# The last token tile's modulated rows u: by Pool, a diagonal matmul and a plain store instead of VectorE, ScalarE and an adding store

## The chip, the cores and the metric

One Trainium2 chip, one core. A core has TensorE (PE, matmuls), VectorE (DVE), ScalarE (ACT), GpSimd (Pool) and SyncE (SP), each with its own instruction queue, and 16 DMA engines. They are ordered by semaphores alone: an instruction waits until a semaphore has reached a value, and instructions and DMAs raise semaphores when they are done. The metric is the time of one execution in microseconds, lower is better.

## What is computed

One layer of a hybrid backbone for 128 context tokens and 512 latent tokens: a modulated projection, three mixers (attention, a recurrence, a long convolution), an output projection with a norm, then a mixture of 16 experts of which each token takes two, and a last norm. The change lies between the first norm and the experts:

```python
xs = layer_norm(ALPHA * xs + g1 * mix, ln1_g[l], ln1_b[l])
u = layer_norm(xs) * (1.0 + sc2) + sh2
xs = layer_norm(ALPHA * xs + g2 * hier_moe(u, *moe_p), ln2_g[l], ln2_b[l])

def hier_moe(u, wg, bg, we, be, w_gate, w_up, w_down):
    g_logits = (jnp.einsum('bld,dg->blg', u, wg) + bg).astype(F32)
    g_idx = jnp.argmax(g_logits, axis=-1)
    ...
    e_logits = (jnp.einsum('bld,de->ble', u, we) + be).astype(F32)
    ...
    h = jax.nn.silu(jnp.einsum('bld,edf->blef', u, w_gate)) * jnp.einsum('bld,edf->blef', u, w_up)
    return jnp.einsum('blef,ble,efd->bld', h, combine, w_down)
```

Context tokens (c = 0) and latent tokens (c = 1) have their own sc2 and sh2.

## The kernel before

**Tiles.** The 640 tokens are TT = 5 tiles of P = 128 rows (tile 0 is context, tiles 1 to 4 latent), D = 1024 wide. The kernel is written engine by engine. The order on each engine is the order of the code, and there is no scheduler.

**Where u goes.** The experts read u row by row, gathered by token number. So each tile's u is written to a table in DRAM, u_scr (640 x 1024), and Pool then gathers the 128 rows of each expert from it with an indirect DMA (L895 in token_rows, into xg). TensorE turns the gathered rows (L1880), ScalarE and VectorE make a high and a low part of them, and the matmuls of the expert follow (L1898). SP's queue loads the experts' weights. Experts 0 and 1 are loaded early, and those of expert 2 wait until the first gather has landed (xg_in).

**How u is made.** X1 is the tile after the first norm, nmr its negative mean, rstd the reciprocal root of its variance, sc2b and sh2b the broadcast 1 + sc2 and sh2. Tiles 0 to 2: two passes on VectorE (L2473, L2474), and a plain store from Pool's queue (L867). Tiles 3 and 4 go another way: early in the stage (near 351 us) ScalarE's queue fills their rows of u_scr with sh2 (L1235). VectorE makes (X1 + nmr) * sc2 in one pass (scaled_rows, L2510) into u2_home[i], ScalarE multiplies by rstd (L1291, raises l1_std), and Pool's queue stores with an adding DMA (L889, raises scat).

```python
for i in range(TT - 2, TT):
    eng.wait_ge(l1_std, 2 * TT + i + 3 - TT)
    eng.dma_start(u_scr[i * P:(i + 1) * P, :], u2_home[i], accum_op=ALU.add).then_inc(scat, 16)
eng.wait_ge(scat, 16 * TT)
eng.wait_ge(slots_rdy, 1)
```

**The routing beside it.** The router's logits aren't made from u but from the rows turned before the second norm is applied: TensorE turns them (L1806), multiplies them with the router's weights (L1842, L1813), and turns the result (L1853, raises lg_mm to 3). VectorE corrects by mean and deviation (LOFF at L2520 and L2521, rr at L2522 for tile 4, by Pool at L880 to L884 for tiles 0 to 3), forms the logits LO (L2547, L2549), and goes on in some 40 small instructions, each waiting for the one before: group, ranks of the experts, the table of chosen experts (L2564, raises onehot). TensorE counts with it (L1859, L1861, raises rank_mm), VectorE makes one-hots of the ranks (L2584), TensorE turns them into token numbers (L1868), and L2599 writes the list tokens (raises slots_rdy to 1), by which Pool gathers. Where TensorE would idle, dense(n) puts n matmuls of 128x512 in between whose result nobody reads (L1833).

**ScalarE's order there:** the deviation of tile 4 (L1260, L1262), the copy of the logits (L1288), the two scalings (L1291), then eight gate_up_high, the high parts of the weights of experts 0 and 1 (L1256).

## Time and profile before

| | us |
|---|---|
| median of 3 runs | 634.61 |
| lowest and highest of them | 634.25, 636.15 |
| the profiled execution | 633.17 |
| its span in the trace | 631.3 |
| TensorE busy in the span | 600.8 (95%) |
| VectorE busy | 440.5 (70%) |
| ScalarE busy | 305.6 (48%) |
| Pool busy | 188.4 (30%) |

The span is the part of the execution that the trace covers. The 1.9 us around it are in every execution. Times in rows are microseconds from the span's start. "Idle before <- releaser" in a row says how long the engine stood still ahead of it and what ended that.

### The profile page before, as it was taken

To read this page: it belongs to the slowest core of one execution; us is meant where nothing else is said; L and a number is where in the kernel's file an instruction comes from. 1 tells how busy PE (TensorE), PEld (TensorE's weight loads), DVE (VectorE), ACT (ScalarE), POOL (GpSimd) and SP (SyncE) were. 2 spreads that over 40 slices of the span, in tenths; PEclk is the share of its full clock that TensorE was granted. 3 is DMA by queue.
4 is the path that set the end of the run, shared out by engine and by line. 5 is a ranking of instruction groups with operands and counts; after the bars stand their busy time and mean duration, and the time that the engine had idled before them with its cause. 6 is when DMAs were issued, how large, how long until landed. Compare 5 with 4: busy or idle time off the path is not lost.

```text
span 631.3 us, 9327 instructions
## 1 busy us (share of the span) xinstructions
PE 600.8 (95%) x3353; PEld 455.3 (72%) x3353; DVE 440.5 (70%) x757; ACT 305.6 (48%) x506; POOL 188.4 (30%) x152
## 2 busy tenths in 40 slices
PE   6899999999999988998999999989999999999994
PEld 2237999999999965557888888747767677676352
DVE  4967766834994654467553499988998877983187
ACT  2748122335344543005795342846565655752354
POOL 1002333345551307041496070421212221321121
PEclk9999999999999999999999999999999999999998
DMA  9985852222221269764980706769999999999788
GB/s 305 387 305 222 305 186 97 101 101 100 101 68 66 92 238 325 303 264 99 290 271 36 294 8 234 280 168 370 393 376 403 390 388 406 374 364 372 291 299 144
DMA packets 40040, 154.89 MB, mean 245 GB/s; under 512 B 7049, under 2 KB 17033, under 8 KB 27451
## 3 DMA queue, kind: packets, MB, share of 16 engines
q1 hardware_dynamic: 27912, 115.41, 50.6%
q10 hardware_dynamic: 5522, 23.48, 9.4%
q0 software_dynamic: 6560, 15.42, 8.3%
q8 instruction: 27, 0.44, 0.3%
q14 instruction: 19, 0.15, 0.1%
HBM read 141.59 MB, written 23.63 MB: 262 GB/s over the span
## 4 chain that ended last, share of the span: by engine, by line
PE 82%; DVE 7%; DMA 5%; ACT 4%; issue 2%; POOL 0%; DVEq 0%; ACTq 0%; POOLq 0%
PE bank L1898 13%; PE bank L1574 12%; PE bank L1575 12%; PE bank L1770 9%; PE bank L1952 8%; PE bank L1410 3%; PE bank L1747 2%; PE bank L1674 2%; PE bank L1880 2%; DMA arena<-in_w_mod 2%; PE bank L1477 2%; PE bank L1625 2%; PE bank L2011 2%; PE bank L1730 2%; DMA u_scr<-arena 1%
## 5 line engine op out<-in xcount | busy, mean ns | idle before, releaser
L772 POOL TENSOR_TENSOR w_low<-arena,w_high 128x1024 fp32r<-128x1024 f32 x22 | 53.6, 2437 | 145.9 <-ACT w_high L971 145.9
L2544 DVE TENSOR_TENSOR gate_up_low<-arena,gate_up_high 128x1024 fp32r<-128x1024 f32 x64 | 75.3, 1221 | 12.3 <-ACT gate_up_high L1256 10.2
L1256 ACT ACTIVATE gate_up_high<-arena 128x1024 fp32r<-128x1024 f32 x64 | 63.9, 1054 | 15.5 <-DMA arena<-in_moe_w_gu 15.5
L971 ACT ACTIVATE w_high<-arena 128x1024 fp32r<-128x1024 f32 x22 | 23.2, 1058 | 87.8 <-PE bank L1575 87.0
L1574 PE MATMUL bank<-u_high,w_high 128*128 128x320 f32 x176 | 56.3, 320 | 1.7 <-DVE u_low L2157 1.7
L1952 PE MATMUL bank<-arena 128*128 128x512 f32 x128 | 57.7, 593 | 0.0
L1575 PE MATMUL bank<-u_high,w_low 128*128 128x320 f32 x176 | 54.4, 309 | 0.0
L1574 PE MATMUL bank<-u_high,w_low 128*128 128x320 f32 x176 | 54.4, 309 | 0.0
L1574 PE MATMUL bank<-u_low,w_high 128*128 128x320 f32 x176 | 54.4, 309 | 0.0
L1575 PE MATMUL bank<-u_low,w_high 128*128 128x320 f32 x176 | 54.4, 309 | 0.0
L1575 PE MATMUL bank<-u_high,w_high 128*128 128x320 f32 x176 | 54.4, 309 | 0.0
L1898 PE MATMUL bank<-gate_up_high,xt_high 128*128 128x512 f32 x128 | 51.4, 402 | 0.5 <-DVE xt_low L2696 0.5
L1898 PE MATMUL bank<-gate_up_low,xt_high 128*128 128x512 f32 x128 | 50.0, 391 | 0.0
L1898 PE MATMUL bank<-gate_up_high,xt_low 128*128 128x512 f32 x128 | 50.0, 390 | 0.0
L902 POOL DMA_INDIRECT y_scr<-arena,store_rows x16 | 17.7, 1108 | 84.2 <-DVE arena L2710 79.7
L1952 PEld LDWEIGHTS bank<-arena 128*128 128x128 f32 x128 | 23.2, 190 | 23.1 <-issue 23.0
L895 POOL DMA_INDIRECT arena<-u_scr,tokens x18 | 19.6, 1087 | 59.1 <-PE bank L1880 49.6
L1574 PEld LDWEIGHTS bank<-u_high,w_high 128*128 128x128 f32 x176 | 33.1, 188 | 2.9 <-DVE u_low L2157 2.6
L1575 PEld LDWEIGHTS bank<-u_high,w_high 128*128 128x128 f32 x176 | 33.1, 188 | 0.2 <-issue 0.2
L1574 PEld LDWEIGHTS bank<-u_low,w_high 128*128 128x128 f32 x176 | 33.0, 188 | 0.0
L1574 PEld LDWEIGHTS bank<-u_high,w_low 128*128 128x128 f32 x176 | 33.0, 188 | 0.0
L1575 PEld LDWEIGHTS bank<-u_low,w_high 128*128 128x128 f32 x176 | 33.0, 188 | 0.0
(442 smaller groups left out, 1396.4 us busy)
## 6 DMA issues: line engine op xcount, KB each, us to landing
arena<-in_moe_w_gu SPq DMA_DIRECT2D x38, 1024.0 KB, 10.1
arena<-in_w_mod SPq DMA_DIRECT2D x24, 1024.0 KB, 6.6
arena<-in_moe_w_down ACTq DMA_DIRECT2D x13, 1024.0 KB
arena<-in_w_in SPq DMA_DIRECT2D x11, 1024.0 KB, 4.8
arena<-in_moe_w_down SPq DMA_DIRECT2D x6, 1024.0 KB
y_scr<-arena SPq DMA_DIRECT2D x11, 512.0 KB, 9.1
arena<-in_x SPq DMA_DIRECT2D x10, 512.0 KB, 9.6
arena<-y_scr SPq DMA_DIRECT2D x10, 512.0 KB, 6.0
```

The source lines that it names most:

```text
L772: G.tensor_tensor(WL[s_][:, :, w], ring[s_][:, :, w], WH[m % 2].bitcast(F), ALU.subtract).then_inc(wl_rdy, 1)
L895: eng.indirect_dma_start(xg[j], None, u_scr, bass.IndirectOffsetOnAxis(ap=which, axis=0), bounds_check=NTOK - 1, oob_is_err=False).then_in ...
L902: eng.indirect_dma_start(y_scr, bass.IndirectOffsetOnAxis(ap=stores[:, n:n + 1], axis=0), yy[n % 2], None, bounds_check=2 * NTOK, oob_is_e ...
L971: S.activation(WH[m % 2], ring[(m // 2) % 2][:, :, (m % 2) * P:(m % 2 + 1) * P], ACT.Copy).then_inc(wh_rdy, 1)
L1256: S.activation(WGH[j][c], raw_gu[s][:, c, :, :], ACT.Copy).then_inc(wgh_rdy, 1)
L1410: last = mm(bank[32 * g:32 * g + 32, :], cond32[k], w[:, 512 * g:512 * (g + 1)], start=(k == 0), stop=(k == KT - 1))
L1574: mm(B[1 + m % 2][:, 0:HALF], w, u[k][:, HALF:NTOK], start=first, stop=end)
L1575: last = mm(B[3 + m % 2][:, 0:HALF], w, u[k][:, 0:HALF], start=first, stop=end)
L1770: last = mm(B[2 * (i % 2) + b][:, :], x[j][:, k, :], w[p][c][:, k % 2, :], start=(k == 0 and q == 0), stop=(k == KT - 1 and q == 2))
L1898: last = mm(B[j][:, :], x[j][:, k, :], w[k // 2][:, k % 2, :], start=(k == 0 and q == 0), stop=(k == KT - 1 and q == 2))
L1952: last = mm(B[4 + b][:, :], hT[j][:, k, :], raw_dn[s][:, k, b * 512:(b + 1) * 512], start=(k == 0), stop=(k == 1))
L2544: tt_(WGL[s][c], raw_gu[s][:, c, :, :], WGH[j][c].bitcast(F), ALU.subtract).then_inc(wgl_rdy, 1)
```

## The change

For tile 4, the last one:

- VectorE's scaled_rows(4) goes. Pool makes (X1 + nmr) * sc2 in two halves of 512 columns, a tensor_scalar and a tensor_tensor for each (raising wcol_rdy to 4 and 5), between its work on the routing's corrections and its store of tile 3.
- ScalarE no longer scales the tile. It scales the 128x128 identity by rstd into root_diag.
- TensorE multiplies root_diag with each half and adds a row of ones times sh2 into the same bank, two matmuls for each half (raising lg_mm to 4 and 5). They stand where dense(4) stood. The next two groups of dense use banks 4 and 5 in place of 2 and 3.
- ScalarE copies each half from its bank to u2_home[4], one before its first gate_up_high and one before its second (raising l1_std to 2 TT + 4).
- SP stores the tile with a plain DMA (raising last_rows_st), ahead of the weights of expert 2. The filling of tile 4's rows of u_scr with sh2 goes, and so ld_late is waited for at 10.
- Pool stores tile 3 with an adding DMA as before, behind its four passes. The first gather waits for the four stores on scat, for last_rows_st, and for slots_rdy.
- Semaphore modc_in is dropped to make room, and cond_rdy counts to 2 in its place.

```diff
--- before.py
+++ after.py
@@ -308,6 +308,7 @@
         U2 = late.take(TT, D)
         YT = [late.take(KT, P) for _ in range(TT)]
         YTF = [y.rearrange("p a b -> p (a b)") for y in YT]
+        root_diag = U2[:, 0, 0:P]
         u2_home = [YTF[2], YTF[3], YTF[4], arena[:, MTH_AT[1]:MTH_AT[1] + D], U2[:, 4, :]]
         wr = Region(WO0 - 1216, 1216)
         WP = wr.take(2, KT, 20)
@@ -476,7 +477,7 @@
         out_st = sem("out_st")
         out_last = sem("out_last")
         scalar_st = sem("scalar_st")
-        modc_in = sem("modc_in")
+        last_rows_st = sem("last_rows_st")
         eo_win = sem("eo_win")
         ld_spec = sem("ld_spec")
         mask_in = sem("mask_in")
@@ -668,6 +669,8 @@
             eng.wait_ge(utl_rdy, KT + TT)
             for e in range(NE):
                 if e == 2:
+                    eng.wait_ge(l1_std, 2 * TT + 4)
+                    eng.dma_start(u_scr[4 * P:5 * P, :], u2_home[4]).then_inc(last_rows_st, 16)
                     eng.wait_ge(xg_in[0], 16)
                 gate_up_weights(e, e % 3, e * D)
                 if e == 0:
@@ -842,7 +845,7 @@
             out_low(3, 0)
             out_low(3, 1)
 
-            eng.wait_ge(ld_late, 16 * 11)
+            eng.wait_ge(ld_late, 16 * 10)
             eng.wait_ge(pv_mm, 40)
             by_row = [P, 2, KT, 20]
             wide = wrt.unsqueeze(1).to_broadcast(by_row)
@@ -883,11 +886,17 @@
             step(G.tensor_tensor(LOFF[:, most], LOFF[:, most], c4x[:, most], ALU.add))
             G.tensor_tensor(rr[:, most], r1s[:, most], rstd[:, most], ALU.mult).then_inc(wcol_rdy, 1)
             after(wcol_rdy)
-            eng.wait_ge(scat, 16 * (TT - 2))
-            for i in range(TT - 2, TT):
-                eng.wait_ge(l1_std, 2 * TT + i + 3 - TT)
-                eng.dma_start(u_scr[i * P:(i + 1) * P, :], u2_home[i], accum_op=ALU.add).then_inc(scat, 16)
-            eng.wait_ge(scat, 16 * TT)
+            eng.wait_ge(l1_var, 2 * TT)
+            eng.wait_ge(yt_mm, 2 * TT)
+            for b in range(2):
+                half = slice(512 * b, 512 * (b + 1))
+                step(G.tensor_scalar(u2_home[4][:, half], X1[:, 4, half], nmr[:, 4:5], None, ALU.add))
+                G.tensor_tensor(u2_home[4][:, half], u2_home[4][:, half], sc2b[:, 1, half], ALU.mult).then_inc(wcol_rdy, 1)
+                after(wcol_rdy)
+            eng.wait_ge(l1_std, 2 * TT + 2)
+            eng.dma_start(u_scr[3 * P:4 * P, :], u2_home[3], accum_op=ALU.add).then_inc(scat, 16)
+            eng.wait_ge(scat, 16 * (TT - 1))
+            eng.wait_ge(last_rows_st, 16)
             eng.wait_ge(slots_rdy, 1)
 
             def token_rows(j, which):
@@ -1231,8 +1240,7 @@
                 for c in range(2):
                     eng.dma_start(dst[:, c, :], mod_scr[c, m * D:(m + 1) * D].partition_broadcast(P)
                                   ).then_inc(ld_late, 16)
-            for i in range(TT - 2, TT):
-                eng.dma_start(u_scr[i * P:(i + 1) * P, :], mod_scr[1, D:2 * D].partition_broadcast(P)).then_inc(ld_late, 16)
+            eng.dma_start(u_scr[3 * P:4 * P, :], mod_scr[1, D:2 * D].partition_broadcast(P)).then_inc(ld_late, 16)
             for a, m in enumerate((2, 1)):
                 for c in range(2):
                     eng.dma_start(WCOL[:, 2 * a + c, :], mod_scr[c, m * D:(m + 1) * D].rearrange("(p k) -> p k", k=KT)
@@ -1286,10 +1294,14 @@
             deviation(TT - 1, 1)
             eng.wait_ge(lg_mm, 2)
             S.activation(LGT, B[1][:, 0:P], ACT.Copy).then_inc(yt_ev, 1)
-            for i in range(TT - 2, TT):
-                eng.wait_ge(u2_rdy, i + 1)
-                S.activation(u2_home[i], u2_home[i], ACT.Copy, scale=rstd[:, i:i + 1]).then_inc(l1_std, 1)
+            eng.wait_ge(u2_rdy, TT)
+            S.activation(root_diag, ident, ACT.Copy, scale=rstd[:, 4:5]).then_inc(l1_std, 1)
+            S.activation(u2_home[3], u2_home[3], ACT.Copy, scale=rstd[:, 3:4]).then_inc(l1_std, 1)
             for c in range(4):
+                if c < 2:
+                    half = slice(512 * c, 512 * (c + 1))
+                    eng.wait_ge(lg_mm, 4 + c)
+                    S.activation(u2_home[4][:, half], B[2 + c][:, :], ACT.Copy).then_inc(l1_std, 1)
                 gate_up_high(0, 0, 0, c)
 
 
@@ -1494,7 +1506,7 @@
             filter_layer(0)
             front_dense(4)
             filter_layer(1)
-            eng.wait_ge(modc_in, 1)
+            eng.wait_ge(cond_rdy, 2)
             front_dense(4)
             eng.wait_ge(filt_sin, 2)
             eng.wait_ge(ld_tables, 64)
@@ -1851,7 +1863,12 @@
             logits(4)
             eng.wait_ge(yt_ev, 2 * TT + 1)
             T.transpose(B[0][:, 0:P], LGT, ident).then_inc(lg_mm, 1)
-            dense(4)
+            eng.wait_ge(l1_std, 2 * TT + 1)
+            for b in range(2):
+                half = slice(512 * b, 512 * (b + 1))
+                eng.wait_ge(wcol_rdy, 4 + b)
+                mm(B[2 + b][:, :], root_diag, u2_home[4][:, half], start=True, stop=False)
+                mm(B[2 + b][:, :], ones[0:1, :], sh2b[0:1, 1, half], start=False, stop=True).then_inc(lg_mm, 1)
 
             eng.wait_ge(wcol_rdy, 2)
             eng.wait_ge(onehot, 1)
@@ -1861,7 +1878,7 @@
                 last = mm(counts[:, a + 1:, :], ones_w, MH[:, a, :].unsqueeze(1).to_broadcast([P, TT - a, NE]),
                           start=False, stop=(a == TT - 1))
             last.then_inc(rank_mm, 1)
-            dense(3)
+            dense(3, (4, 5))
             for q in range(2 * TT):
                 if q % TT == 0:
                     eng.wait_ge(onehot, 2 + q // TT)
@@ -1959,7 +1976,7 @@
             for i in range(TT):
                 last = mm(B[7][:, P + 2 * NE:P + 3 * NE], RO[:, TT + i, :], SECOND[:, i, :], start=(i == 0), stop=(i == TT - 1))
             last.then_inc(rank_mm, 1)
-            dense(5)
+            dense(5, (4, 5))
             rows_transposed(0, 0)
             dense(2, (4, 5))
             for n in range(NE):
@@ -2040,8 +2057,8 @@
             eng.wait_ge(ld_const, 16)
             eng.wait_ge(cond_rdy, 1)
             step(stt(sig, sig, 1.0, cond, ALU.add, ALU.mult))
-            ts_(cond, sig, 0.5, None, ALU.mult).then_inc(modc_in, 1)
-            after(modc_in)
+            ts_(cond, sig, 0.5, None, ALU.mult).then_inc(cond_rdy, 1)
+            eng.wait_ge(cond_rdy, 2)
 
             magic = 1.5 * 2.0 ** 23
             hi = 6.28125
@@ -2466,7 +2483,7 @@
 
                 c = 1 if i else 0
                 if i == 0:
-                    eng.wait_ge(ld_late, 16 * 11)
+                    eng.wait_ge(ld_late, 16 * 10)
                 if i < TT - 2:
                     eng.wait_ge(l1_std, 2 * i + 2)
                     step(V.reciprocal(rstd[:, i:i + 1], rstd[:, i:i + 1]))
@@ -2511,8 +2528,6 @@
 
             scaled_rows(3).then_inc(u2_rdy, 1)
             after(u2_rdy)
-            eng.wait_ge(yt_mm, 2 * TT)
-            step(scaled_rows(4))
             eng.wait_ge(l1_std, 2 * i + 2)
             V.reciprocal(rstd[:, i:i + 1], rstd[:, i:i + 1]).then_inc(u2_rdy, 1)
             after(u2_rdy)
```

Pool's queue between the routing's corrections (L882 to L884 before) and the first gather; arena is SBUF, u_scr the table in DRAM. Before:

```order
L882 TENSOR_TENSOR arena<-arena 128x80 [waits pool_step]
L883 TENSOR_TENSOR arena<-arena 128x80 [waits pool_step]
L884 TENSOR_TENSOR arena<-arena 128x4 [waits pool_step]
L889 DMA u_scr<-arena 128x1024 [waits l1_std,scat,wcol_rdy]
L889 DMA u_scr<-arena 128x1024 [waits l1_std]
L895 DMA arena<-u_scr,tokens 128x1024 [waits slots_rdy,scat]
```

Now:

```order
L885 TENSOR_TENSOR arena<-arena 128x80 [waits pool_step]
L886 TENSOR_TENSOR arena<-arena 128x80 [waits pool_step]
L887 TENSOR_TENSOR arena<-arena 128x4 [waits pool_step]
L893 TENSOR_SCALAR arena<-arena 128x512 [waits yt_mm,l1_var,wcol_rdy]
L894 TENSOR_TENSOR arena<-arena 128x512 [waits pool_step]
L893 TENSOR_SCALAR arena<-arena 128x512 [waits wcol_rdy]
L894 TENSOR_TENSOR arena<-arena 128x512 [waits pool_step]
L897 DMA u_scr<-arena 128x1024 [waits l1_std,wcol_rdy]
L904 DMA arena<-u_scr,tokens 128x1024 [waits slots_rdy,last_rows_st,scat]
```

Four passes stand ahead of the store of tile 3, and one of the two adding stores is gone.

VectorE in the same stretch, from the negative mean of tile 4 to the logits. Before:

```order
L2506 TENSOR_SCALAR arena<-arena 128x1 [waits vector_step]
L2510 SCALAR_TENSOR_TENSOR arena<-arena 128x1024 [waits l1_var]
L2510 SCALAR_TENSOR_TENSOR arena<-arena 128x1024 [waits yt_mm,u2_rdy]
L2517 RECIPROCAL arena<-arena 128x1 [waits l1_std,vector_step]
L2520 SCALAR_TENSOR_TENSOR arena<-arena 128x20 [waits wcol_rdy,u2_rdy]
L2521 SCALAR_TENSOR_TENSOR arena<-arena 128x20 [waits vector_step]
L2522 TENSOR_TENSOR arena<-arena 128x1 [waits vector_step]
L2547 TENSOR_TENSOR arena<-bank,arena 128x100 [waits lg_mm,ld_attn,vector_step]
L2549 TENSOR_TENSOR arena<-arena 128x100 [waits vector_step]
```

Now:

```order
L2523 TENSOR_SCALAR arena<-arena 128x1 [waits vector_step]
L2527 SCALAR_TENSOR_TENSOR arena<-arena 128x1024 [waits l1_var]
L2532 RECIPROCAL arena<-arena 128x1 [waits l1_std,u2_rdy]
L2535 SCALAR_TENSOR_TENSOR arena<-arena 128x20 [waits wcol_rdy,u2_rdy]
L2536 SCALAR_TENSOR_TENSOR arena<-arena 128x20 [waits vector_step]
L2537 TENSOR_TENSOR arena<-arena 128x1 [waits vector_step]
L2562 TENSOR_TENSOR arena<-bank,arena 128x100 [waits lg_mm,ld_attn,vector_step]
L2564 TENSOR_TENSOR arena<-arena 128x100 [waits vector_step]
```

One pass of 128x1024 is gone, and the rest stands as it did.

TensorE between the logits' last transpose and the counts. Before:

```order
L1813 MATMUL bank<-arena 128x20 x7
L1853 MATMUL bank<-arena 128x128 [waits yt_ev]
L1833 MATMUL bank<-arena 128x512 x4
L1859 MATMUL bank<-chosen,upper_whole 128x96 [waits onehot,wcol_rdy]
L1861 MATMUL bank<-chosen,ones_whole 128x80
```

Now:

```order
L1825 MATMUL bank<-arena 128x20 x7
L1865 MATMUL bank<-arena 128x128 [waits yt_ev]
L1870 MATMUL bank<-arena 128x512 [waits wcol_rdy,l1_std]
L1871 MATMUL bank<-arena 128x512
L1870 MATMUL bank<-arena 128x512 [waits wcol_rdy]
L1871 MATMUL bank<-arena 128x512
L1876 MATMUL bank<-chosen,upper_whole 128x96 [waits onehot,wcol_rdy]
```

Four matmuls that wait for Pool and ScalarE stand where four stood that waited for nothing.

## Rows read from the trace of the kernel before

**Rows 1.** The page: the span, and the chain that ended last by engine.

```profile
span 631.3 us, 9327 instructions
...
PE 82%; DVE 7%; DMA 5%; ACT 4%; issue 2%; POOL 0%; DVEq 0%; ACTq 0%; POOLq 0%
```

**Rows 2.** The chain in order of time, 396 to 425: start, duration, what.

```profile
406.83 0.78 POOL u_scr L889
407.61 8.44 DMA u_scr<-arena
...
416.08 0.04 POOLq L895
...
416.93 4.28 DMA arena<-u_scr,tokens
```

**Rows 3.** VectorE in order of time: start, duration, line, operation, operands, count, idle before.

```profile
403.16 2.61 DVE L2510 SCALAR_TENSOR_TENSOR arena<-arena 128x1024 f32<-128x1024 f32 x2
405.81 0.16 DVE L2517 RECIPROCAL arena<-arena 128x1 f32<-128x1 f32 x1
406.00 0.24 DVE L2520 SCALAR_TENSOR_TENSOR arena<-arena 128x20 f32<-128x20 f32 x1
...
406.56 0.16 DVE L2522 TENSOR_TENSOR arena<-arena 128x1 f32<-128x1 f32 x1
406.75 0.26 DVE L2547 TENSOR_TENSOR arena<-bank,arena 128x100 f32<-128x100 f32 x1
407.05 0.27 DVE L2549 TENSOR_TENSOR arena<-arena 128x100 f32<-128x100 f32 x1
...
415.44 0.23 DVE L2599 TENSOR_SCALAR tokens<-arena 128x16 int32<-128x16 f32 x1
```

**Rows 4.** Pool and VectorE side by side, 399 to 402, in order of time.

```profile
399.79 1.45 DVE L2501 SCALAR_TENSOR_TENSOR arena<-arena 128x1024 f32<-128x1024 f32 x1
...
399.81 0.35 POOL L881 TENSOR_TENSOR arena<-arena 128x80 f32<-128x80 f32 x1
400.24 1.18 POOL L882 TENSOR_TENSOR arena<-arena 128x80 f32<-128x80 f32 x1
```

**Rows 5.** ScalarE in order of time, 404 to 415.

```profile
404.63 0.29 ACT L1262 ACTIVATE arena<-arena 128x1 f32<-128x1 f32 x1
...
405.13 2.18 ACT L1291 ACTIVATE arena<-arena 128x1024 f32<-128x1024 f32 x2
407.21 7.67 ACT L1256 ACTIVATE gate_up_high<-arena 128x1024 fp32r<-128x1024 f32 x8
```

**Rows 6.** TensorE in order of time; an f32 matmul is two records.

```profile
406.25 0.31 PE L1853 MATMUL bank<-arena 128*128 128x128 f32 x1
406.39 3.60 PE L1833 MATMUL bank<-arena 128*128 128x512 f32 x8
410.75 0.20 PE L1859 MATMUL bank<-chosen,upper_whole 128*128 128x96 bf16 x1 [0.76 <-DVE chosen L2564]
```

**Rows 7.** Pool's groups by form: count, busy us, mean ns, idle before.

```profile
L803 POOL TENSOR_TENSOR arena<-arena 128x1024 f32<-128x1024 f32 x8 | 18.8, 2355 | 21.6 <-DMA arena<-in_rpb 21.5
...
L814 POOL TENSOR_TENSOR arena<-arena 128x256 f32<-128x256 f32 x10 | 7.3, 728 | 43.0 <-DVE arena L2351 43.0
...
L784 POOL TENSOR_SCALAR arena<-arena 128x1280 f32<-128x1280 f32 x1 | 1.3, 1267 | 0.1
```

**Rows 8.** Pool and VectorE at 111 us, in order of time.

```profile
111.66 2.42 POOL L772 TENSOR_TENSOR w_low<-arena,w_high 128x1024 fp32r<-128x1024 f32 x1 [5.17 <-ACT w_high L971]
...
111.78 2.31 DVE L2296 TENSOR_TENSOR arena<-arena 128x4 f32<-128x4 f32 x1
```

**Rows 9.** Landing of L867's plain and L889's adding stores; busy us by stretch, clock, DMA share.

```profile
DMA to landing us min/median/max: 2.9/3.4/7.1
...
DMA to landing us min/median/max: 6.3/7.4/8.4
...
405.00:410.00 5.00, 4.99 (x22) 2.72 (x21) 4.42 (x18) 5.00 (x6) 1.83 (x2) 1.00 1.02 351
410.00:415.00 5.00, 3.57 (x22) 1.63 (x22) 4.54 (x14) 4.98 (x7) 0.00 (x0) 1.00 0.97 178
```

## Prediction

> **What bounds the kernel now.** I read the page first, then the chain of waits through the routing stage, then each engine's rows of that stage in order of time. The page shows a kernel that TensorE bounds over most of its span: PE holds 82% of the chain that ended last [rows 1]. The change touches none of that bulk. It lies in the 20 us in which TensorE has nothing large to do, because the first expert's tokens aren't known yet. There the chain [rows 2] goes from ScalarE's scaled rows to Pool's adding store (issued at 407.61), to its landing 8.44 us later, and to the gather of the first expert's rows, which starts at 416.93 and lands 4.28 us later. Everything behind the gather waits for it: TensorE's transposes, the expert matmuls, and the next weights on SP's queue, which wait for the gather too. So a shift of the first gather passes on in full, and the forecast is the question of when that gather starts.
>
> Two things must be there before it: u in DRAM (semaphore scat) and the token list (slots_rdy). The chain names only the later one. VectorE's rows [rows 3] show the other: L2599 writes the list from 415.44 for 0.23 us, so it is there at **415.67**. The store's landing at 407.61 + 8.44 = 416.05 is only **0.38 us** behind it. That is the most that any faster store can give while VectorE's chain stays where it is.
>
> **What leaves VectorE.** One pass of 128x1024 (the second of the two at L2510, 2 x 1.30 us in one row [rows 3]) goes. The reciprocal L2517 stood at 405.81 behind it. It now waits for ScalarE's root, which starts at 404.63 and takes 0.29 us [rows 5], so it runs at about 404.97 to 405.13. That is 0.8 us earlier. The gain isn't kept: L2547 reads the transposed logits, and TensorE makes them at 406.25 to 406.56, behind a queue of its own that the change doesn't touch [rows 6]. VectorE came there at 406.75 in before. So without any new wait the list could come 0.2 us sooner at most.
>
> **What comes to Pool, and what it does to VectorE.** Pool gets four passes of 128x512: twice a tensor_scalar, then a tensor_tensor. The price of a tensor_tensor: 2355 ns at 1024 elements and 728 at 256 [rows 7], a slope of 2.12 ns, so 512 cost 1.27 us. For the tensor_scalar the nearest row is 1267 ns at 1280 elements with two constants [rows 7], about 0.53 us at 512. Here the scalar is a column of SBUF, which no row of Pool shows, so its upper end is the tensor_tensor's 1.27 us and its lower end 0.53. I take the lower, since the row is the same instruction with as many operands streamed. Sum: 2 x (0.53 + 1.27) = 3.6 us, up to 5.1.
>
> These passes aren't free for VectorE, though it waits on none of them by semaphore. At 111.66 Pool starts a tensor_tensor of 2.42 us, and VectorE's addition of 4 elements, started at 111.78, takes 2.31 us: it ends when Pool's does [rows 8]. Its like takes 0.16 (L2522 has one element [rows 3]). It works the other way as well: Pool's L882 starts at 400.24, takes 1.18 us in place of L881's 0.35, and ends 0.15 us after VectorE's 128x1024 pass (399.79 + 1.45 = 401.24) [rows 4]. An instruction of VectorE with two tensors in SBUF and one of Pool take turns, each holding off the other for its whole length. The routing chain consists of such small instructions.
>
> The page "SBUF — State Buffer" of the Trainium skill, section "SBUF: two separate sides", calls it an exclusive lock that whoever starts first keeps for the whole instruction, and exempts a VectorE instruction with only one tensor in SBUF. The 2.31 us above agree with the lock. By the exemption L2547, which reads one tensor from PSUM, would pass beside Pool, which moves the result between my two ends below and not beyond them.
>
> So the new order of time from 403 on, by these durations. Pool is ready at about 403.2, when the negative mean is there, as is VectorE's first L2510 (403.16 [rows 3]), which holds it until 404.45. Tensor_scalar until 405.0, tensor_tensor to 406.3, tensor_scalar to 406.9, tensor_tensor 407.0 to 408.3. VectorE's L2520 is ready at 405.2 and is held to 406.3. L2521 and L2522 get in between Pool's passes one at a time, and whichever is next at 407.0 is held to 408.3. If that is L2549 (started 407.05 in before, ended 407.32), it ends at about 408.4: **1.1 us** late. If it is still L2522, then L2522, L2547 and L2549 follow one another after 408.3 (0.1 + 0.3 + 0.3 us) and L2549 ends at about 408.95: **1.6 us** late. I take **1.3**. From there on nothing of Pool runs beside the chain, and its rest takes what it took: list at 415.67 + 1.3 = 417.0.
>
> **TensorE.** dense(4), 3.60 us of filling from 406.39 [rows 6], goes. In its place stand four matmuls of 128x512 in f32, as dense's were, so 3.6 us again, in two pairs of 1.8: from 406.6 (its first half is ready at 406.3) to 408.4, and from 408.4 to 410.2. The counts behind them waited for the one-hot until 410.75, which now comes 1.3 us later. So the matmuls are hidden with 1.8 us of room, and TensorE idles about 1.8 us there in place of 0.76. Without that cover they would be on the path with their whole length.
>
> **The store of the last tile.** ScalarE: diagonal 405.2 to 405.5, tile 3 scaled to 406.6 (1.05 us, as in before [rows 5]). It copies half 0 at 408.4 to 409.0, then one gate_up_high (1.0), then half 1 at 410.3 to 410.9. The other seven gate_up_high end at 417.6 in place of 414.88 [rows 5]. Their first reader on VectorE comes after the gather's issue, the first tile's pieces are done by 414, and the exponential behind them is needed only experts later: nothing. SP has nothing ahead of the plain store (its next weights wait for the gather), so it goes out at 410.9. The weights in front of it have drained by then (351 GB/s in 405 to 410, 178 in 410 to 415 [rows 9]). The plain stores of the other tiles land in 2.9 to 7.1 us, median 3.4 [rows 9], so **413.8 to 418.0**, and I take 414.5, since one adding store runs beside it.
>
> **The adding store of tile 3** stood ready at 406.28 and was issued at 406.83. Now it stands behind Pool's four passes: 408.3. The two adding stores landed in 6.3 and 8.4 us [rows 9], sharing the engines with each other and the weights. That gives 414.6 with the shorter and 416.7 with the longer. I take the shorter, as there is now one and the weights are out. Both stores are in before the list at 417.0: the list is what ends last.
>
> **Sum.** Gather released at 417.0 in place of 416.05: **+0.9 us** (+0.7 to +1.2 over the two ends of VectorE's delay). The other edits are at nothing: one preset of 512 KB fewer on ScalarE's queue near 352, under the output matmuls, the renamed wait at the start (same producer, same place), and the dense groups moved to other banks. The profiled execution took 633.17 us with a span of 631.3, so the same execution would take 634.1. The median of the runs shown lies 1.44 us above it, at 634.61, which gives **635.5 us**.
>
> **Rivals.** (a) *No turns taken:* VectorE's small instructions slip through Pool's passes. Then the list comes at 415.5 and both stores are in before it: -0.5 us, 634.1. For: Pool's L881, started 0.02 us behind VectorE's long pass, took only 0.35 us [rows 4]. Against: the 2.31 us for 4 elements [rows 8], the plainest row of the argument. (b) *Pool's passes run long*, slower than before. With the column operand at 1.27 us each, Pool ends 1.5 us later, at 409.8, and VectorE's delay grows to 2.6 to 3.1, the gather's to 2.2 to 2.7: 637.1. It passes 0.3% when Pool's sum exceeds about 4.6 us. Half 1's matmuls then end at 411.6, still before the one-hot. (c) *A store ends last:* the plain store at 7.1 us lands at 418.0, +1.95 us, 636.6. It decides once it takes over 6.1 us. For: it crosses an adding store; against: two of the three plain stores took 3.4 or less. (d) *The route is swapped but the gather isn't moved:* the store's 0.4 us and VectorE's delay cancel, 634.6; it needs a delay of only 0.4 us.
>
> The page "GPSIMD Engine Reference" of the Trainium skill, section "Elementwise — side-by-side cycle accounting", gives some 2.6 cycles of 1.2 GHz an element with two inputs and 1.03 for the simplest bodies. Worked out from it as an estimate, the four passes take 2 x (1.11 + 0.44) = 3.1 us without overhead, and the delay of VectorE would be about 0.5 us less, with a result near 635.0.
>
> **Chances.** Forecast (its +0.7 to +1.2, with 0.2 us to either side for the order in which the two engines take turns) 0.56, (a) 0.12, (b) 0.11, (c) 0.09, (d) 0.12. A measurement of this kernel tells about 0.3% from no change, 1.9 us. The forecast, (a) and (d) lie within it. (b) mostly and (c) in half its cases lie beyond, 0.15 with some of the forecast's tail. 0.04 is left for a gain beyond what any step here allows. The range takes in (a) and (b) with the 0.4 us by which the fastest of the runs shown lies below its median: 633.7 to 637.6.
>
> **What would show it.** Right: L2520's successor on VectorE (a pass of 20 elements, 0.24 us now) lasting over 1 us and ending with a tensor_tensor of Pool, Pool's passes summing to 3.6 us behind a held first one, onehot about 1.3 us later, and the wait before the gather naming VectorE's tokens and not a store. Wrong: routing instructions at their old 0.2 us beside Pool's passes, a tensor_scalar far over 0.53 us, or a store's landing as the gather's releaser. The granted clock falling in the 1.8 us of idle TensorE (it is 1.00 in the rows of this stretch [rows 9]) would add time that no term here holds.

## The result and the profile after

The change made the kernel slower. Over 8 executions each, the changed kernel took 639.69 us (median, 638.14 to 641.01) and the kernel before 634.46 (633.58 to 637.58), a ratio of 1.0065 with a 95% interval of 1.0042 to 1.0088. The forecast was 635.5 us with a range up to 637.6, "no change that can be told" as the likeliest: it was wrong. The profiled execution took 639.83 us with a span of 637.8, against 633.17 and 631.3.

The chain of waits through the routing stage of the changed kernel (start, duration, what):

```profile
403.74 2.59 POOL arena L893
406.33 0.07 issue
406.40 1.28 POOL arena L894
407.68 0.14 issue
407.81 2.01 PE bank L1870 x2
409.83 2.00 PE bank L1871 x2
411.83 2.00 PE bank L1870 x2
413.83 2.00 PE bank L1871 x2
415.83 0.19 PE bank L1876
...
423.51 4.31 DMA arena<-u_scr,tokens
```

The first gather starts at 423.51 and not at 416.93 [rows 2], 6.6 us later, and the span grew by 6.5. So in these two profiled executions the loss is all ahead of that gather. Neither a store nor VectorE holds it: the chain goes through Pool's first half and then through the four new matmuls, 2.0 us each where dense's took 0.9 [rows 6].

TensorE in order of time shows why. Its last transpose of the logits stands at 406.67, which is 0.42 us later than in before. That part came in ahead of this stage (in the profiled execution of the changed kernel TensorE's clock was also below full between 20 and 40, at 0.95 and 0.88, and in that of before it was not), and I leave it out of the account below.

```profile
406.67 0.30 PE L1865 MATMUL bank<-arena 128*128 128x128 f32 x1
407.81 2.01 PE L1870 MATMUL bank<-arena 128*128 128x512 f32 x2 [0.84 <-POOL arena L894]
409.76 2.07 PE L1871 MATMUL bank<-arena 1*128 1x512 f32 x2
411.76 2.08 PE L1870 MATMUL bank<-arena 128*128 128x512 f32 x2
413.76 2.07 PE L1871 MATMUL bank<-arena 1*128 1x512 f32 x2
415.77 0.26 PE L1876 MATMUL bank<-chosen,upper_whole 128*128 128x96 bf16 x1
415.83 0.40 PE L1878 MATMUL bank<-chosen,ones_whole 128*128 128x80 bf16 x5
416.08 5.47 PE L1845 MATMUL bank<-arena 128*128 128x512 f32 x6
```

The counts (L1876) had their one-hot from 412.13 on (L2579 below) and started at 415.77, behind the matmuls. The filling behind them (L1845, six records) took 5.47 us against 2.8 at full clock. The busy time by stretch names the cause. Its columns are the stretch, its length, busy us of PE, PEld, DVE, ACT and POOL with their instructions, the granted clock, the DMA share and GB/s:

```profile
400.00:405.00 5.00, 4.86 (x90) 4.28 (x88) 4.70 (x7) 4.97 (x11) 4.38 (x6) 1.00 1.00 416
405.00:410.00 5.00, 4.16 (x20) 2.50 (x21) 3.39 (x14) 2.02 (x5) 4.73 (x4) 0.78 0.87 364
410.00:415.00 5.00, 5.00 (x6) 1.25 (x6) 3.30 (x11) 1.54 (x2) 1.62 (x2) 0.50 0.53 75
415.00:420.00 5.00, 5.00 (x12) 2.14 (x12) 2.67 (x6) 4.13 (x5) 0.00 (x0) 0.50 0.41 135
420.00:425.00 5.00, 4.14 (x22) 1.69 (x21) 2.19 (x7) 4.80 (x7) 1.19 (x2) 0.85 0.00 0
```

**TensorE's clock fell from 2.4 to 1.2 GHz** between 405 and 410 and stood at half through 410 to 420, in a stretch in which before had 1.00 throughout ([rows 9] up to 415, and its trace up to 425). It isn't one bad execution: the mean granted clock of the eight, each over its whole span, was 0.982 to 0.988.

Pool and VectorE in the same stretch:

```profile
403.74 2.58 POOL L893 TENSOR_SCALAR arena<-arena 128x512 f32<-128x512 f32 x1 [0.31 <-DVE arena L2523]
406.40 1.27 POOL L894 TENSOR_TENSOR arena<-arena 128x512 f32<-128x512 f32 x1
407.77 1.56 POOL L893 TENSOR_SCALAR arena<-arena 128x512 f32<-128x512 f32 x1
409.42 1.26 POOL L894 TENSOR_TENSOR arena<-arena 128x512 f32<-128x512 f32 x1
```

```profile
405.65 0.24 DVE L2535 SCALAR_TENSOR_TENSOR arena<-arena 128x20 f32<-128x20 f32 x1
...
407.40 0.38 DVE L2564 TENSOR_TENSOR arena<-arena 128x100 f32<-128x100 f32 x1
...
408.03 0.46 DVE L2550 TENSOR_TENSOR arena<-arena 128x20 f32<-128x20 f32 x1
...
409.75 1.03 DVE L2574 TENSOR_TENSOR arena<-arena 128x80 f32<-128x80 f32 x1
...
411.89 0.24 DVE L2579 TENSOR_TENSOR chosen<-arena 128x80 bf16<-128x80 f32 x1
```

Three instructions of the routing chain are longer than their like (0.27, 0.18 and 0.24 us), by 0.11, 0.28 and 0.79 us. The first and the last end 0.1 us behind Pool's two tensor_tensors (407.67 and 410.68). L2535 took its usual 0.24 us, although Pool's first tensor_scalar ran until 406.32. Pool's two tensor_scalars took 2.58 us (held until VectorE's long pass ended at 404.87) and 1.56, not 0.53.

The stores, once they were issued, were quick. Pool's adding store of tile 3 (issued at 410.99) and SP's plain store of tile 4 (issued at 416.49):

```profile
DMA to landing us min/median/max: 5.4/5.4/5.4
...
DMA to landing us min/median/max: 2.6/2.6/2.6
```

The plain store landed at 419.1, and the list was there only at 422.55.

**Account of the 6.6 us**, with the 0.4 of shift taken out (6.2): the counts came 4.6 us late (415.77 against 410.75), of which VectorE's one-hot explains 1.1 (412.13 against 410.60) and the slow, late matmuls 3.5. From the counts to the list another 1.9 us, the filling matmuls at half clock. Less the 0.4 us by which the store had been later than the list in before.

### The profile page after: what moved, and what is told of

Same layout as the page of the kernel before. It is cut to its first block, busy times and chain, and to the rows that moved or that the text cites. A ratio compares the mean times of both kernels' runs of the same rounds, so it can differ in the third digit from the quotient of the medians.

```text
span 637.8 us, 9332 instructions
## 1 busy us (share of the span) xinstructions
PE 608.4 (95%) x3353; PEld 457.4 (72%) x3353; DVE 440.7 (69%) x756; ACT 306.5 (48%) x508; POOL 192.9 (30%) x155
## 4 chain that ended last, share of the span: by engine, by line
PE 82%; DVE 8%; DMA 3%; ACT 3%; issue 2%; POOL 1%; DVEq 0%; POOLq 0%; ACTq 0%
PE bank L1915 13%; PE bank L1586 12%; PE bank L1587 12%; PE bank L1782 9%; PE bank L1969 8%; PE bank L1422 3%; PE bank L1759 2%; PE bank L1686 2%; PE bank L1897 2%; PE bank L1489 2%; DMA arena<-in_w_mod 2%; PE bank L1637 2%; PE bank L2028 2%; PE bank L1742 2%; PE bank L1503 1%
```

## The experiments

The first theory: the idle 0.84 us ahead of the first new matmul, behind small matmuls, let the clock fall. The rival: something in the new work does. "One-row" in the table means that a matmul sums over one row of both operands (`1*128`, `1x512` in its row), "full" that it sums over 128, and "gap" an idle stretch ahead of the new or held matmuls. "Clock" is the range of the mean granted clock over the executions of a kernel. The kernel before has 0.987 to 0.997 in these series, and a ratio is to the kernel before on the same chip. The clock is a mean over the whole span, so it also holds what happened elsewhere: in the profiled executions of a4_const, b2_one_row and d1_pool_rows it was below full between 20 and 40 too, in code that b2 and d1 share with the kernel before. Only a trace tells where it fell, and there is one for each kernel (two for the changed one).

| kernel | TensorE in the stretch | median us | ratio, 95% | clock |
|---|---|---|---|---|
| changed | gap, one-row | 639.69 | 1.0065 (1.0042 to 1.0088) | 0.982 to 0.988 |
| a6_again (the same) | gap, one-row | 639.87 | 1.0078 (1.0054 to 1.0101) | 0.982 to 0.988 |
| a1_fill | filled, one-row | 635.83 | 1.0020 (0.9998 to 1.0042) | 0.987 to 0.996 |
| a2_full | gap, full | 636.32 | 1.0007 (0.9985 to 1.0028) | 0.991 to 0.997 |
| a5_two_ops | short gap, full | 635.59 | 1.0002 (0.9976 to 1.0028) | 0.988 to 0.996 |
| c1_vector_rows | no gap, one-row | 635.55 | 1.0005 (0.9976 to 1.0034) | 0.982 to 0.994 |
| c2_vector_rows_full | no gap, full | 635.06 | 1.0005 (0.9986 to 1.0023) | 0.989 to 0.997 |
| b1_gap | gap, dense | 634.91 | 1.0013 (0.9990 to 1.0036) | 0.986 to 0.996 |
| b2_one_row | no gap, one-row | 636.92 | 1.0029 (1.0008 to 1.0050) | 0.982 to 0.991 |
| b3_gap_one_row | gap, one-row | 638.21 | 1.0056 (1.0029 to 1.0084) | 0.980 to 0.991 |
| d1_pool_rows | no gap, dense | 637.98 | 1.0050 (1.0027 to 1.0074) | 0.989 to 0.997 |
| a4_const | filled, full | 637.11 (one execution) | | 0.990 |

**a1_fill: a filling matmul where TensorE stood idle.**

```diff
+            dense(1, (4, 5))
             eng.wait_ge(l1_std, 2 * TT + 1)
             for b in range(2):
```

> The changed kernel with one filling matmul (0.9 us, two records) ahead of the wait for Pool's first half, where TensorE stood idle 0.84 us. Theory 1 (the idle stretch behind the small matmuls of the logits let the clock fall to 1.2 GHz): the clock stays at 1.00 through 405 to 425, the four new matmuls take 3.6 us, not 8.0, the counts wait for the one-hot again, and the gather starts about 1.1 to 1.5 us later than in the kernel before: 635.6 to 636.1. Theory 2 (the clock falls with the new matmuls or with Pool's passes whatever stands ahead of them): it falls again, and the time stays near 639.5. Theory 3 (the lateness of Pool's second half alone costs it): the clock stays, yet the time is over 638.

635.83 us, a mean clock of 0.992 or more in nine of ten executions, the gather at 417.36. An idle stretch of 0.78 us ahead of the second half stayed, and both one-row matmuls. Theory 1 passed, and it looked settled. What ends last there is the plain store (issued at 412.40, landed at 416.45), 0.4 us behind the list. So in this trace Pool's lateness alone, at full clock, costs about a microsecond (the gather is 0.4 us later than in before, and the transpose of the logits 0.8 us earlier).

**b1_gap: the same idle stretch in the kernel before.**

```diff
+            eng.wait_ge(l1_std, 2 * TT + 2)
             dense(4)
```

> The kernel before with its dense(4) held until ScalarE has scaled both tiles, at about 407.3, so that TensorE stands idle some 0.75 us behind the logits' transpose as in the changed kernel, and nothing else is altered. Theory 1: the clock falls to 1.2 GHz at about 407, dense(4) takes near 8 us, the counts come 4 to 5 us late: 638 to 640. Theory 2 (the new matmuls or Pool's passes are needed for it): the clock stays at 1.00, dense(4) ends at 411.0 instead of 409.99, and the counts come 0.2 us late: 634.4 to 635.0.

TensorE stood idle for 0.80 us and dense(4) then took 3.70 us at full clock. 634.91 us, ratio 1.0013 with 1 inside the interval. **Theory 1 fell**: the gap by itself does nothing that can be told.

**c1_vector_rows: Pool's passes out, VectorE makes the rows again, TensorE's new work stays.**

```diff
-                step(G.tensor_scalar(u2_home[4][:, half], X1[:, 4, half], nmr[:, 4:5], None, ALU.add))
-                G.tensor_tensor(u2_home[4][:, half], u2_home[4][:, half], sc2b[:, 1, half], ALU.mult).then_inc(wcol_rdy, 1)
...
+            eng.wait_ge(yt_mm, 2 * TT)
+            step(scaled_rows(4))
...
+            eng.wait_ge(u2_rdy, TT)
-                eng.wait_ge(wcol_rdy, 4 + b)
```

> The changed kernel with Pool's four passes taken out and tile 4's scaled rows made by VectorE again in one pass, as in the kernel before. The diagonal, the row of ones and the plain store stay. Theory 1: the first half is there at about 406.3, before TensorE is done with the logits, so there is no idle stretch and no fall of the clock. VectorE's chain is as in the kernel before, the plain store lands at about 415, and the gather waits for the list: 0.3 to 0.5 us faster than before, 634.0 to 634.3. Theory 2 with the new matmuls as the cause (a fall with TensorE's new work): near 638. A plain store that takes over 5 us to land would end last and give 635 or more.

TensorE has no idle stretch here, and yet, in its order of time:

```profile
406.33 0.31 PE L1858 MATMUL bank<-arena 128*128 128x128 f32 x1
406.56 1.13 PE L1863 MATMUL bank<-arena 128*128 128x512 f32 x2
407.61 1.12 PE L1864 MATMUL bank<-arena 1*128 1x512 f32 x2
408.66 1.86 PE L1863 MATMUL bank<-arena 128*128 128x512 f32 x2
410.45 2.07 PE L1864 MATMUL bank<-arena 1*128 1x512 f32 x2
```

The first pair runs at full clock and the second at half: the clock fell in the middle of busy work. The executions spread from 633.54 to 640.72, with mean clocks from 0.982 to 0.994. My expectation of no fall was wrong, and the spread pointed at the new matmuls, of which every second has a single row of weights. The median of 635.55 is that of before: one-row matmuls without an idle stretch ahead of them cost nothing here that can be told, and only the spread and the trace speak.

**d1_pool_rows: Pool's part alone, in the kernel before.** Pool's four passes ahead of the adding stores, VectorE's pass out, ScalarE scaling behind Pool.

```diff
+                step(G.tensor_scalar(u2_home[4][:, half], X1[:, 4, half], nmr[:, 4:5], None, ALU.add))
+                G.tensor_tensor(u2_home[4][:, half], u2_home[4][:, half], sc2b[:, 1, half], ALU.mult).then_inc(wcol_rdy, 1)
...
+                if i == TT - 1:
+                    eng.wait_ge(wcol_rdy, 5)
...
-            step(scaled_rows(4))
```

> The kernel before with tile 4's scaled rows made by Pool's four passes, ahead of its two adding stores. ScalarE's scaling, the adding store and dense(4) stay. This is Pool's part alone. The clock stays at 1.00, since dense(4) waits for nothing (theory 1), or falls if Pool's passes were its cause (theory 2, 637 or more). Pool ends at about 410.3 by the 1.56 and 1.27 us of the changed kernel's passes, ScalarE at 411.4, the adding store of tile 4 goes out at 412 and lands 5 to 6.5 us later at 417 to 418.5, past the list (about 416.9, VectorE held for 1.2 us in all): the gather starts 1 to 2.5 us late, 635.6 to 637.0.

The clock stayed at 1.00 through 400 to 415, so Pool's passes do not pull it down there. It fell behind that, to 0.75 in 415 to 420 and 0.90 in 420 to 425, with no one-row matmul in the stretch; the gather was waiting for a store until 420.40, and TensorE then waited for the rows, so it cost nothing there. The one-hot was there at 411.74 against 410.60, so VectorE's chain came 1.1 us late, though it had one long pass less. The time, 637.98, is beyond my 637.0. In the profiled execution (637.89) that is the adding store of tile 4, which took 8.57 us to land and not 5 to 6.5:

```profile
411.83 8.57 DMA u_scr<-arena
```

Adding stores kept to the 8.4 us of [rows 9], and being one store behind the other seems to have mattered more than the emptier engines (DMA share 0.63 and 0.69, against 1.02 and 0.97).

**c2_vector_rows_full and a2_full: all 128 rows in place of one.**

```diff
-                mm(B[2 + b][:, :], ones[0:1, :], sh2b[0:1, 1, half], start=False, stop=True).then_inc(lg_mm, 1)
+                mm(B[2 + b][:, :], ident, sh2b[:, 1, half], start=False, stop=True).then_inc(lg_mm, 1)
```

> The kernel of c1_vector_rows with the row-of-ones matmul (one row of weights, sh2 from one row) replaced by the identity times the broadcast sh2, a matmul over all 128 rows with the same result. In c1 the clock fell at about 409 though TensorE never stood idle. Theory A (a matmul of one row counts for little activity, and the fall needs weak work, not idleness): the clock stays at 1.00 in 405 to 425, the four matmuls take 3.6 us, the gather waits for the list or the plain store, whichever is later, at about 415.5 on the time axis of the kernel before: 0.3 to 0.6 us less than before, and no execution near 638. Theory B (the fall comes from waiting for the work in this stage, whatever the matmuls hold): the clock falls as in c1, with executions spread to 638 and more.

> The changed kernel with the same replacement, and nothing ahead of the wait for Pool's first half: the idle 0.84 us behind the logits' small matmuls stays. Theory A with the idle stretch as a cause of its own: the clock still falls at about 407.8, since it fell there ahead of the first one-row matmul, but it comes back sooner than after 13.7 us: 637.5 to 639. Theory A with one-row matmuls as the whole cause: no fall, 635.6 to 636.2. Theory B: as the changed kernel, 639.5.

The result is the same sum, since sh2b holds sh2 in every row. In c2 the stretches up to 415 are at 1.00, the four matmuls took 3.7 us, and the list was there at 415.37. In a2, with the whole of the idle time:

```profile
407.62 1.10 PE L1870 MATMUL bank<-arena 128*128 128x512 f32 x2 [0.84 <-POOL arena L894]
408.55 1.02 PE L1871 MATMUL bank<-arena 128*128 128x512 f32 x2
410.54 1.12 PE L1870 MATMUL bank<-arena 128*128 128x512 f32 x2 [0.97 <-POOL arena L894]
411.50 1.02 PE L1871 MATMUL bank<-arena 128*128 128x512 f32 x2
412.36 0.21 PE L1876 MATMUL bank<-chosen,upper_whole 128*128 128x96 bf16 x1
```

There are two idle stretches of 0.84 and 0.97 us and no fall. In ten executions no mean clock was under 0.991, against ten of ten at 0.988 or less for a6_again, whose code differs in this one line, and the two intervals lie apart (up to 1.0028, from 1.0054). **With this one line the kernel loses 3.6 us less** by the medians (636.32 against 639.87) and 4.5 by the ratios, of a loss of 4.1 to 5.2. But the line is one of two conditions: with the one-row matmuls left in, the filling matmul of a1_fill did as much (635.83). Each alone brings nearly all of it back, so they are not two gains to be added. My expectation for a2 had leant to the fall coming anyway, since in the changed kernel's profile the clock had fallen with the first new matmul. That was wrong.

c2 has everything that could make the change a gain: no Pool passes, the full matmul, a plain store. It came out at 1.0005 (0.9986 to 1.0023), no faster than before. The 0.3 to 0.6 us that I expected aren't in its trace either, and I had expected no execution near 638, where one took 638.73. The plain store was issued at 410.53 and took 5.3 us, so a store still ended last, 0.4 us behind the list as in before:

```profile
416.70 1.11 POOL L897 DMA_INDIRECT arena<-u_scr,tokens  x1 [8.08 <-DMA u_scr<-arena]
```

And the clock fell in 415 to 420 (0.66), behind the list, with no one-row matmul in the stretch: the filling there took until 421.7, some 0.7 us after the rows had landed at about 420.9. No kernel of this series beats the kernel before.

**b2_one_row and b3_gap_one_row: the suspects in the kernel before.** In both, dense(4) becomes four one-row matmuls. b3 holds them as b1 did.

```diff
+            eng.wait_ge(l1_std, 2 * TT + 2)
-            dense(4)
+            for b in range(4):
+                mm(B[2 + b % 2][:, :], ident[0:1, :], consts[0:1, 2 * KT:2 * KT + 512], start=True, stop=True)
```

> The kernel before with its dense(4) made of matmuls over one row of weights (their result is read by nobody, so the output is the same). No wait and no Pool pass is added. Theory A: the clock falls near 408 to 410 in many executions though TensorE is never idle longer than before. The counts come up to 3 us late, and executions lie at 634 to 639. Theory B or the idle stretch as the only cause: clock and time as before.

> The kernel before with both of the suspects on TensorE and nothing else: dense(4) made of one-row matmuls, and held until ScalarE has scaled both tiles (about 0.8 us idle). No Pool pass, no plain store. Apart, the hold did nothing (b1_gap) and the one-row matmuls let the clock fall in a part of the executions (b2_one_row, 636.9). If weak work adds up over the logits' small matmuls, the hold and the one-row matmuls, the clock falls in nearly every execution, as in the changed kernel: 638 to 641, mean granted clock 0.990 or less. If the changed kernel's loss needed Pool's lateness on top, it stays near b2_one_row's 637.

The eight records of the replaced dense(4), of b2 and then of b3 (dense itself: 3.60 us):

```profile
409.08 5.58 PE L1855 MATMUL bank<-arena 1*128 1x512 f32 x8
```

```profile
407.23 5.00 PE L1856 MATMUL bank<-arena 1*128 1x512 f32 x8 [0.80 <-ACT arena L1291]
```

b2: 1.0029, b3: 1.0056. No Pool pass, no diagonal and no plain store is in either. The gap seems to add to the one-row matmuls (636.92 against 638.21, and more executions at 0.989 or less: six and eight of ten), though the intervals overlap, and it does nothing that can be told with full matmuls behind it. b3 comes near the changed kernel and shows that the loss of the clock can arise on TensorE alone. Its executions at 0.990 and 0.991 went against my "nearly every".

**a4_const and a5_two_ops: what a pass of Pool costs.** a4 is the changed kernel with filling and the full matmul, and with a constant in place of the column.

```diff
-                step(G.tensor_scalar(u2_home[4][:, half], X1[:, 4, half], nmr[:, 4:5], None, ALU.add))
+                step(G.tensor_scalar(u2_home[4][:, half], X1[:, 4, half], -0.01, None, ALU.add))
```

> The changed kernel with a filling matmul ahead of the wait, the full matmul for sh2, and Pool's tensor_scalar with a constant (-0.01) in place of the column of negative means, so that tile 4's u lacks its own mean's subtraction. It prices the column operand: if the column is what makes it dear, the pass of 128x512 takes 0.53 us as scaled from 1267 ns at 1280 elements (against 1.56 with the column), Pool ends 2 us sooner, and the idle stretches of TensorE vanish. If the price lies elsewhere (a fixed cost, contention with the DMAs), it stays near 1.5.

The unheld pass took 1.49 us (second half, 1.56 with the column). So the column isn't what makes it dear. Its clock was 1.00 through 400 to 440 and below full between 20 and 40 (0.89 and 0.77), and the time of a single execution, 637.11, says nothing more. Then a5, which is a2_full with a second operation that changes nothing:

```diff
+                step(G.tensor_scalar(u2_home[4][:, half], X1[:, 4, half], nmr[:, 4:5], 1.0, ALU.add, ALU.mult))
```

> The kernel of a2_full with Pool's tensor_scalar written with two operations (add the column, multiply by 1.0) in place of one. In a4_const the constant operand cost 1.49 us against 1.56 for the column, so the column isn't what makes the pass dear. Theory C (on Pool a tensor_scalar of one operation is the dear form and one of two operations the cheap one, as L790 with 3469 ns and L784 with 1267 ns at 1280 elements): the pass takes 0.5 to 0.6 us, Pool ends about 2 us sooner than in a2_full, TensorE is idle under 0.3 us ahead of the first half, and the time is 0.5 to 1.5 us less than that of a2_full. Theory D (L784's price came from elsewhere): the pass stays at 1.5 us and the time at a2_full's 636.

```profile
403.02 1.70 POOL L893 TENSOR_SCALAR arena<-arena 128x512 f32<-128x512 f32 x1 [0.31 <-DVE arena L2523]
404.81 1.27 POOL L894 TENSOR_TENSOR arena<-arena 128x512 f32<-128x512 f32 x1
406.18 0.69 POOL L893 TENSOR_SCALAR arena<-arena 128x512 f32<-128x512 f32 x1
406.96 1.27 POOL L894 TENSOR_TENSOR arena<-arena 128x512 f32<-128x512 f32 x1
```

**With two operations the pass takes 0.69 us in place of 1.56** (0.5 to 0.6 expected). TensorE is hardly idle ahead of its halves, and 635.59 against 636.32 us goes the way expected, though the intervals overlap. Two executions stand at 638.22 and 638.62 with clocks of 0.989 and 0.988, without a trace. VectorE is held here too, in single instructions of 1.18 us (L2535, 0.24 otherwise) and 1.13 (L2564), both of which end with a tensor_tensor of Pool. The list was there at 416.71, and the wait ahead of the gather names it.

**a6_again: the changed kernel a second time.**

> The changed kernel itself, for comparison on the same chip and for a second trace: where the clock falls in another execution. The kernels of this series that hold full-row matmuls stayed above a mean granted clock of 0.99. Expected: 638 to 641 again, mean clock 0.990 or less, the fall somewhere between 407 and 411 and its return between 415 and 422.

```profile
407.25 1.10 PE L1870 MATMUL bank<-arena 128*128 128x512 f32 x2 [0.84 <-POOL arena L894]
408.27 1.72 PE L1871 MATMUL bank<-arena 1*128 1x512 f32 x2
410.17 2.07 PE L1870 MATMUL bank<-arena 128*128 128x512 f32 x2 [0.18 <-POOL arena L894]
```

Here the first new matmul still runs at full clock, and the fall comes in the one-row matmul behind it. The place differs between the two profiled executions; the fall is in both. The expectation puts all kernels with full matmuls above 0.99, which is not so: c2 has two executions at 0.989.

**What stays open.** In the changed kernel's profile the clock fell together with the first new matmul, before any one-row matmul had run. Up to that point a2_full does the same work, and its profile shows no fall there. One of its ten executions has a mean clock of 0.991, and so do executions of the kernel before, so a short fall there may occur in it as well. No trace of mine caught one, and I did not settle whether the one-row matmuls start the fall in every execution or in some only keep it from ending. The clock also fell behind the list in d1 and c2, where no one-row matmul stands in the stretch, so one row is not the only way to lose it. And the line that a2 changes makes both operands full at once; which of the two counts is not tested.

## Why the prediction was wrong, point by point

- **The bound and the window of 0.4 us.** Right as a bound. c2, with the most favourable form of the change, gained nothing that can be told, and its plain store ended 0.4 us behind the list as the adding one had.
- **TensorE: "3.6 us again", hidden with 1.8 us of room.** This is the step that failed. The four matmuls took 8.0 us, with the last ending at 415.8 and not at 410.2. I took dense's price for them because the shape was alike. At full clock that was nearly right even for the one-row ones (2.1 and 2.2 us a pair in a1_fill); what was wrong was that the clock would stay, where two of the four have one row and a wait stands ahead of them. I also treated dense(4) as filling that something else could replace. With the full matmul (a2_full) the four took 3.9 us in two pairs around the second wait and the kernel came out at 1.0007, inside the range.
- **The clock.** The prediction named its fall as what no term held, gave it no chance of its own, and left it out of the range. It should have been the rival on the slow side: the stretch holds 32 matmuls with 32 columns of weights and 8 with a result 20 columns wide ahead of dense(4), then a wait, then new work whose rows had not been looked at.
- **Pool's tensor_scalar, 0.53 us, upper end 1.27.** Mis-sized, with an upper end too low. It measured 1.56 free and 2.58 held. The row that it was scaled from has two operations (and by its own length gives 0.51 us at 512). The view of the changed kernel's groups has both forms at 1280 elements side by side:

```profile
L793 POOL TENSOR_SCALAR arena<-arena 128x1280 f32<-128x1280 f32 x1 | 3.5, 3472 | 0.0
...
L787 POOL TENSOR_SCALAR arena<-arena 128x1280 f32<-128x1280 f32 x1 | 1.3, 1271 | 0.1
```

  The first is the one-operation form (2.7 ns an element, which gives 1.39 us at 512 and fits a4's 1.49) and the second the one with two. The trace of before has the same pair (L790, 3469 ns, and L784, 1267), and the prediction used only the second. The tensor_tensor, 1.27 us, was right to the hundredth. Pool ended at 410.7 (410.3 without the shift) in place of 408.3.
- **VectorE held by Pool.** Right, and nearly right in size: forecast 1.1 to 1.6 us, measured 1.1 in the changed kernel and 1.1 in d1. But it did not fall where the order of time had put it. L2535 to L2537 went past in Pool's long first pass with no delay (0.24, 0.24 and 0.16 us), and the later instructions were held, by 0.11, 0.28 and 0.79 us, the first and the last by Pool's tensor_tensors. So "each holding off the other for its whole length" was too strong: a tensor_scalar with one operation was held by VectorE's long pass and let most of VectorE's small ones through.
- **Adding store of tile 3, landing 6.3 us.** 5.4, right. It was issued at 411.0, later than forecast, with Pool. **Plain store, 2.9 to 7.1 us, taken 3.6.** 2.6 in the changed kernel, and 5.75 in a2_full, where the two stores run side by side (413.19 to 418.94) and it ended last, 1.9 us behind the list. So rival (c) is what a2_full shows once the clock holds, and a store ended last in a1_fill (4.05 us), a4_const (4.3) and c2 (5.3) as well: "the list is what ends last" held only in a5_two_ops, in the changed kernel, and in the others whose matmuls ran at half clock.
- **Rival (b)**, Pool's passes long, was half of what happened (Pool over 4.6 us, TensorE late by it), with the wrong consequence: I had half 1's matmuls ending ahead of the one-hot still. **(a)** is out as a whole: turns are taken with the tensor_tensors.

## What to carry to other kernels

Before work on TensorE takes the place of filling matmuls, look at the rows of its operands and not only at the shape of its result: here two matmuls with one row of weights, alike in time at full clock (1.12 us for two records against 1.02), cost 3.6 us by the clock that full rows, or one filling matmul ahead of them, would have kept. The identity times a broadcast tile gives the same sum. Price an instruction of Pool from a row with the same number of operations, and count its tensor_tensors also as held time of VectorE. A mean clock over a whole execution says that it fell, and only rows in order of time say where. A wait of 0.8 us on TensorE was harmless with full matmuls behind it (b1, a2) and not with one-row ones (the changed kernel, b3), so it is the whole stretch that has to be read.

## What the runs showed of the hardware that I had not expected

- The clock fell to 1.2 GHz in the midst of busy matmuls (c1, between 408.7 and 410.5, no idle stretch). With one-row matmuls in the stretch all 18 executions of the changed kernel had a mean granted clock of 0.988 or less, and replacing them by 128-row matmuls (a2), or putting one filling matmul ahead (a1, nine of ten executions), brought it back to the values of before. Leaving them out doesn't rule a fall out: 0.66 in 415 to 420 in c2, 0.75 in d1.
- On Pool a tensor_scalar of 128x512 with one operation takes 1.56 us (1.49 with a constant), and with two operations 0.69 us.
- Beside Pool's one-operation tensor_scalar VectorE's instructions with two inputs mostly kept their 0.16 to 0.24 us (L2535 to L2537; L2550 took 0.46), and beside its tensor_tensor they were held to its end (L2574 1.03 us, and L2535 1.18 in a5).
- An adding store of 512 KB landed after 5.2 to 5.6 us where no second adding store was near (eight traces), and after 8.1 to 8.6 as the second of two (before, b1, b2, b3, d1). A plain one took 2.6 us where the adding one had landed, or landed less than 1 us later (changed, a6, c1), and 4.05 to 5.75 beside it (a1, a2, a4, a5, c2).
